# A two-block transformer kernel on one core: wider right sides for thin products, and an expert scatter in two passes, one block later

## What is computed

```python
for layer in range(DEPTH):
    mod = c @ w_ada[layer] + b_ada[layer]
    sh_a, sc_a, g_a, sh_f, sc_f, g_f = [m[:, None, :] for m in jnp.split(mod, 6, -1)]
    h = x * (1.0 + sc_a) + sh_a
    ...
    f = _swiglu(...) if layer % 2 == 0 else _moe(...)
    x = _layer_norm(DEEPNORM_ALPHA * x + (1.0 + g_f) * f, ln_g[layer, 1], ln_b[layer, 1])

def _moe(h, w_router, b_router, wg, wu, wd):     # top 2 of 8 experts, gates = their softmax
    ...
    for e in range(N_EXPERTS):
        out = out + gates[:, e:e + 1].astype(t.dtype) * _swiglu(t, wg[e], wu[e], wd[e])
```

## Time and profile before

| | |
|---|---|
| three runs | 2732.01, 2730.3, 2724.32 us; median 2730.3 |
| profiled execution | 2731.76 us; its span 2730.0 us |
| mean granted clock | 0.979 |
| PE, DVE, ACT busy | 97%, 80%, 56% |

### The profile page before, as it was taken

The page is one execution under the profiler, slowest core; times in us unless marked ns, Lnnn a source line. Parts: engine busy times, 40 slices in busy tenths (PEclk is TensorE's granted clock), DMA queues, the critical chain, the costliest instruction groups (busy, mean ns, idle before and its releaser), DMA issues.

```text
span 2730.0 us, 37737 instructions
## 1 busy us (share of the span) xinstructions
PE 2643.8 (97%) x15664; PEld 2346.4 (86%) x15664; DVE 2186.1 (80%) x2466; ACT 1519.5 (56%) x1567; POOL 50.8 (2%) x83
## 2 busy tenths in 40 slices
PE   6989999989999999999999999999999999999998
PEld 5879988878888888888888799998899999998898
DVE  6978767788888888888888889975487788954777
ACT  3533335557767777766777654544454554444554
POOL 2000000100000000000000000000000000000000
PEclk9989989989999999999999999999999998999999
DMA  8659954489999999999999953454555533444453
GB/s 315 228 203 328 359 203 162 120 311 369 356 342 360 347 356 353 359 348 353 350 356 350 330 178 109 146 173 142 174 193 189 172 115 132 155 154 169 156 186 116
DMA packets 376000, 669.85 MB, mean 245 GB/s; under 512 B 26761, under 2 KB 199439, under 8 KB 370959
## 3 DMA queue, kind: packets, MB, share of 16 engines
q1 hardware_dynamic: 358336, 662.55, 69.0%
q10 hardware_dynamic: 17487, 4.83, 0.7%
HBM read 663.13 MB, written 4.19 MB: 244 GB/s over the span
## 4 chain that ended last, share of the span: by engine, by line
PE 86%; DVE 8%; ACT 3%; issue 2%; DMA 1%; POOL 0%; ACTq 0%; DVEq 0%; POOLq 0%; SPq 0%
PE PS L444 24%; PE PS L446 24%; PE PS L445 24%; PE PS L544 2%; DVE LO L439 2%; DVE AR L721 2%; PE PS L2517 2%; PE PS L1674 2%; ACT HI L430 1%; DVE AR L2807 1%; PE PS L1911 1%; PE PS L1948 1%; PE PS L2403 1%; PE PS L2394 1%; PE PS L749 1%
## 5 line engine op out<-in xcount | busy, mean ns | idle before, releaser
L439 DVE TENSOR_TENSOR LO<-RAW,HI 128x2048 fp32r<-128x2048 f32 x410 | 930.6, 2274 | 221.2 <-ACT HI L430 220.8
L430 ACT ACTIVATE HI<-RAW 128x2048 fp32r<-128x2048 f32 x410 | 780.3, 1904 | 325.6 <-PE PS L446 287.2
L444 PE MATMUL PS<-X1H,HI 128*128 128x256 f32 (+1 forms) x2128 | 611.2, 287 | 7.2 <-DVE X1L L584 4.2
L445 PE MATMUL PS<-X1L,HI 128*128 128x256 f32 (+1 forms) x2128 | 605.2, 284 | 0.0
L446 PE MATMUL PS<-X1H,LO 128*128 128x256 f32 (+1 forms) x2128 | 604.8, 284 | 0.0
L444 PE MATMUL PS<-HI,X1H 128*128 128x512 f32 x1056 | 431.3, 408 | 0.9 <-DVE LO L439 0.4
L444 PEld LDWEIGHTS PS<-X1H,HI 128*128 128x128 f32 (+1 forms) x2128 | 409.4, 192 | 12.4 <-issue 9.8
L446 PE MATMUL PS<-HI,X1L 128*128 128x512 f32 x1056 | 413.8, 392 | 0.0
L445 PE MATMUL PS<-LO,X1H 128*128 128x512 f32 x1056 | 412.9, 391 | 0.0
L445 PEld LDWEIGHTS PS<-X1L,HI 128*128 128x128 f32 (+1 forms) x2128 | 409.4, 192 | 2.1
L446 PEld LDWEIGHTS PS<-X1H,LO 128*128 128x128 f32 (+1 forms) x2128 | 409.1, 192 | 0.8
(11 more groups left out here) (390 smaller groups left out, 2845.4 us busy)
## 6 DMA issues: line engine op xcount, KB each, us to landing
RAW<-in_w_in_dram SPq DMA_DIRECT2D x66, 1024.0 KB, 5.4
RAW<-in_expert_w_gate_dram SPq DMA_DIRECT2D x66, 1024.0 KB, 5.3
RAW<-in_expert_w_up_dram SPq DMA_DIRECT2D x64, 1024.0 KB, 5.3
RAW<-in_expert_w_down_dram SPq DMA_DIRECT2D x62, 1024.0 KB, 5.5
RAW<-in_ffn_w_up_dram SPq DMA_DIRECT2D x55, 1024.0 KB, 5.5
AR<-in_expert_w_down_dram SPq DMA_DIRECT2D x50, 1024.0 KB, 5.6
AR<-in_expert_w_up_dram SPq DMA_DIRECT2D x48, 1024.0 KB, 5.9
AR<-in_expert_w_gate_dram SPq DMA_DIRECT2D x46, 1024.0 KB, 5.5
```

Source lines behind the costliest of these rows:

```text
L430: a.activation(HI[:, n % NH, 0:size(i)], raw_at(i), ACT.Copy).then_inc(*hi.up(i))
L439: v.tensor_tensor(LO[:, m % NH, 0:n], raw_at(i), HI[:, m % NH, 0:n].bitcast(F32), ALU.subtract).then_inc(*lo.up(i))
L444: t.matmul(o, lh, rh, start=first, stop=False)
L445: t.matmul(o, lh, rl, start=False, stop=False)
```

## The change

`pe_ada_sum` takes all 128 columns of ones instead of one, and `gates` takes 128 columns of the tile `U` from where its 8 begin instead of those 8; the columns read are the first ones, as before. In the expert stage the gate values leave the one-hot matrix: only `PP` is built and turned (one buffer `PPT`, fp32r), the result `YE` (one buffer) is split into `YH` by ACT and `YL` by DVE, a quarter is two fp32r passes, and DVE multiplies with the gate value as it adds. The quarters move to blocks b = 2 to 5, the turn to the expert's own last block, and the hidden rows keep 2 slots instead of 3.

```diff
@@ pe_ada_sum
-            z = t.matmul(PS[:, bank, at + j:at + j + 1], SUMMED[n][:, 128 * j:128 * j + 128], ones[:, 0:1], start=True,
-                         stop=True)
+            z = t.matmul(PS[:, bank, at + j:at + j + 128], SUMMED[n][:, 128 * j:128 * j + 128], ones, start=True, stop=True)
@@ dve_select
-            v.tensor_scalar(PP[:, s_, k, :], iota, RP[:, k, x:x + 1], None, ALU.is_equal)
-            z = v.tensor_scalar(PG[:, s_, k, :], iota, RP[:, k, x:x + 1], GG[:, k, x:x + 1], ALU.is_equal, ALU.mult)
+            z = v.tensor_scalar(PP[:, s_, k, :], iota, RP[:, k, x:x + 1], None, ALU.is_equal)
@@ pe_turn, act_turn
+        t.wait_ge(*(dve_moe("gather", x + 1, 1) if x < 7 else dve_moe("scatter", 6, 3)))
+        turn(t, [(PS[:, 7, 128 * k:128 * k + 128], PP[:, x % 2, k, :]) for k in range(2)]).then_inc(*pe_moe.up("turn", x))
...
+        if x > 0:
+            a.wait_ge(*pe_moe("scatter", x - 1, 3))
+        a.activation(PPT[:, :], PS[:, 7, 0:256], ACT.Copy).then_inc(*act_moe.up("turn", x))
@@ pe_scatter
-        if q == 0:
-            t.wait_ge(*dve_moe("y", x))
-        if x < 7:
-            t.wait_ge(*(dve_moe("scatter", x, q - 1) if q else act_moe("turn", x + 1)))
-        t.matmul(PS[:, scatter_bank(x, q), :], PGT[:, x % 2, 128 * k:128 * k + 128], YE[:, x % 2, ns], start=True,
-                 stop=True).then_inc(*pe_moe.up("scatter", x, q))
+        if q == 0 or (x, q) == (7, 1):
+            t.wait_ge(*dve_moe("ylo", x, q if x == 7 else 1))
+            t.wait_ge(*act_moe("turn", x))
+        elif x < 7:
+            t.wait_ge(*dve_moe("scatter", x, q - 1))
+        places = PPT[:, 128 * k:128 * k + 128]
+        t.matmul(PS[:, scatter_bank(x, q), :], places, YH[:, ns], start=True, stop=False)
+        t.matmul(PS[:, scatter_bank(x, q), :], places, YL[:, ns], start=False, stop=True).then_inc(
+            *pe_moe.up("scatter", x, q))
@@ dve_scatter
-        v.tensor_tensor(X[:, k, ns], X[:, k, ns], PS[:, scatter_bank(x, q), :], ALU.add).then_inc(
-            *dve_moe.up("scatter", x, q))
+        v.scalar_tensor_tensor(X[:, k, ns], PS[:, scatter_bank(x, q), :], GG[:, k, x:x + 1], X[:, k, ns], ALU.mult,
+                               ALU.add).then_inc(*dve_moe.up("scatter", x, q))
@@ pe_between (dve_between the same)
-        if x > 0 and 1 <= b <= 4 and after == "g":
-            pe_scatter(t, x - 1, b - 1)
+        if x > 0 and 2 <= b <= 5 and after == "g":
+            pe_scatter(t, x - 1, b - 2)
...
-        if x < 7 and (b, after) == (6, "u"):
-            pe_turn(t, x + 1)
+        if (b, after) == (6, "u"):
+            pe_turn(t, x)
@@ act_hidden_moe (slots n % 3 become n % 2)
-        if n > 2:
-            a.wait_ge(*used(CH[f"moe{(n - 3) // 7}d"][2 * ((n - 3) % 7) + 1]))
+        if n > 1:
+            a.wait_ge(*used(CH[f"moe{(n - 2) // 7}d"][2 * ((n - 2) % 7) + 1]))
@@ act_moe_program
             if 0 < n < 56:
                 split_hi(a)
                 split_hi(a)
+                if b == 0:
+                    act_y(a, x - 1)
@@ dve_moe_program
             if x < NEXP:
                 split_lo(v)
+                if x > 0 and b == 1:
+                    dve_y_lo(v, x - 1)
@@ dve_y, act_y, dve_y_lo
-        if x > 1:
-            v.wait_ge(*pe_moe("scatter", x - 2, 3))
+        if x > 0:
+            v.wait_ge(*pe_moe("scatter", x - 1, 3))
...
+            v.tensor_tensor(YE[:, ns], PS[:, 5 + nb, :], GB2[:, ns], ALU.mult).then_inc(*dve_moe.up("y", x, nb))
+    def y_parts(x):
+        return ((0, slice(0, 512)), (1, slice(512, 1024))) if x == 7 else ((1, slice(0, 1024)),)
+    def act_y(a, x):
+        for nb, ns in y_parts(x):
+            a.wait_ge(*dve_moe("y", x, nb))
+            a.activation(YH[:, ns], YE[:, ns], ACT.Copy).then_inc(*act_moe.up("yhi", x, nb))
+    def dve_y_lo(v, x):
+        for nb, ns in y_parts(x):
+            v.wait_ge(*act_moe("yhi", x, nb))
+            v.tensor_tensor(YL[:, ns], YE[:, ns], YH[:, ns].bitcast(F32), ALU.subtract).then_inc(*dve_moe.up("ylo", x, nb))
@@ gates
-                    z = t.matmul(PS[:, 6 + k, 0:8], src[:, c % 4 if j == 2 else c, 128 * k:128 * k + 128],
-                                 WG[:, l, 8 * j + c, :], start=first and n == 0, stop=last and n == len(part) - 1)
+                    o = 192 * l + 8 * (8 * j + c)
+                    z = t.matmul(PS[:, 6 + k, 0:128], src[:, c % 4 if j == 2 else c, 128 * k:128 * k + 128],
+                                 U[:, o:o + 128], start=first and n == 0, stop=last and n == len(part) - 1)
```

More of the change, by code:

```diff
@@ L252, in emit_program @@
     WR = sb("WR", [128, 8, 8])
+    PPT = sb("PPT", [128, 256], F32R)
     PS = ctx.enter_context(nc.psum_tensor("PS", [128, 8, 512], F32))
@@ L1787, in emit_program @@
     m1, den2, CNT = ar(8272, 2), ar(8274, 2), ar(8280, 8)
-    PP, PG, PGT = ar(8448, 2, 2, 128), ar(8960, 2, 2, 128), ar(9472, 2, 256)
+    PP = ar(8448, 2, 2, 128)
     SGm, HFm = ar(9984, 2, 512), ar(11008, 2, 512)
-    YE = ar(12032, 2, 1024)
+    YE = ar(12032, 1024)
     GB2, LG2, LB2 = ar(14080, 1024), ar(15104, 1024), CST[:, C_DEC:C_DEC + 1024]
@@ L1795, in emit_program @@
     GL = X1L[:, :, :].rearrange("p a b -> p (a b)").rearrange("p (s c n) -> p s c n", s=2, c=8)
-    RHm = X2H[:, :, :].rearrange("p a b -> p (a b)").rearrange("p (s c n) -> p s c n", s=4, c=4)
-    RLm = X2L[:, :, :].rearrange("p a b -> p (a b)").rearrange("p (s c n) -> p s c n", s=4, c=4)
+    RHm = X2H[:, 0:4, :].rearrange("p a b -> p (a b)").rearrange("p (s c n) -> p s c n", s=2, c=4)
+    RLm = X2L[:, 0:4, :].rearrange("p a b -> p (a b)").rearrange("p (s c n) -> p s c n", s=2, c=4)
+    YH, YL = [t_[:, 4:8, :].rearrange("p a b -> p (a b)") for t_ in (X2H, X2L)]
     def pe_router(t):
@@ L1928, in pe_turn @@
     def pe_turn(t, x):
-        if x:
-            t.wait_ge(*dve_moe("gather", x, 1))
-        turn(t, [(PS[:, 7 if x else 6, 128 * k:128 * k + 128], PG[:, x % 2, k, :]) for k in range(2)]).then_inc(*pe_moe.up("turn", x))
+        t.wait_ge(*(dve_moe("gather", x + 1, 1) if x < 7 else dve_moe("scatter", 6, 3)))
+        turn(t, [(PS[:, 7, 128 * k:128 * k + 128], PP[:, x % 2, k, :]) for k in range(2)]).then_inc(*pe_moe.up("turn", x))
     def act_turn(a, x):
         a.wait_ge(*pe_moe("turn", x))
-        if x > 1:
-            a.wait_ge(*pe_moe("scatter", x - 2, 3))
-        a.activation(PGT[:, x % 2, :], PS[:, 7 if x else 6, 0:256], ACT.Copy).then_inc(*act_moe.up("turn", x))
+        if x > 0:
+            a.wait_ge(*pe_moe("scatter", x - 1, 3))
+        a.activation(PPT[:, :], PS[:, 7, 0:256], ACT.Copy).then_inc(*act_moe.up("turn", x))
     def scatter_bank(x, q):
@@ L1973, in act_between @@
             act_gather(a, x + 1, 1)
-        if x < 7 and (b, after) == (6, "u"):
-            act_turn(a, x + 1)
+        if (b, after) == (6, "u"):
+            act_turn(a, x)
     def dve_between(v, x, b, after):
-        if x > 0 and 1 <= b <= 4 and after == "g":
-            dve_scatter(v, x - 1, b - 1)
+        if x > 0 and 2 <= b <= 5 and after == "g":
+            dve_scatter(v, x - 1, b - 2)
         if x < 7 and (b, after) == (0, "g"):
@@ L1990, in pe_moe_program @@
         pe_gather(t, 0, 1)
-        pe_turn(t, 0)
         for n in range(7 * NEXP + 1):
@@ L2021, in pe_down @@
             if x > 0 and b == 0 and half == 0:
-                t.wait_ge(*dve_moe("y", x - 1))
+                t.wait_ge(*dve_moe("y", x - 1, 1))
             for nb, c in ((0, 0), (0, 1), (1, 0), (1, 1)):
                 ns, q = slice(512 * nb, 512 * nb + 512), 2 * half + c
-                z = mm3(t, PS[:, 5 + nb, :], RHm[:, n % 3, q, :], RLm[:, n % 3, q, :], hi_of(i)[:, c, ns],
+                z = mm3(t, PS[:, 5 + nb, :], RHm[:, n % 2, q, :], RLm[:, n % 2, q, :], hi_of(i)[:, c, ns],
                         lo_of(i)[:, c, ns], b == 0 and q == 0, b == 6 and q == 3)
@@ L2041, in act_hidden_moe @@
         a.wait_ge(*pe_moe("hid", n))
-        if n > 2:
-            a.wait_ge(*used(CH[f"moe{(n - 3) // 7}d"][2 * ((n - 3) % 7) + 1]))
-        a.activation(RHm[:, n % 3], PS[:, 4, :].rearrange("p (c n) -> p c n", c=4), ACT.Copy).then_inc(
+        if n > 1:
+            a.wait_ge(*used(CH[f"moe{(n - 2) // 7}d"][2 * ((n - 2) % 7) + 1]))
+        a.activation(RHm[:, n % 2], PS[:, 4, :].rearrange("p (c n) -> p c n", c=4), ACT.Copy).then_inc(
             *act_moe.up("hid", n))
@@ L2048, in dve_hidden_moe @@
         v.wait_ge(*act_moe("hid", n))
-        v.tensor_tensor(RLm[:, n % 3], PS[:, 4, :].rearrange("p (c n) -> p c n", c=4), RHm[:, n % 3].bitcast(F32),
+        v.tensor_tensor(RLm[:, n % 2], PS[:, 4, :].rearrange("p (c n) -> p c n", c=4), RHm[:, n % 2].bitcast(F32),
                         ALU.subtract).then_inc(*dve_moe.up("hidlo", n))
@@ L2058, in act_moe_program @@
         act_gather(a, 0, 1)
-        act_turn(a, 0)
         for n in range(7 * NEXP + 1):
@@ L2168, in emit_program @@
     WB2 = [ar(2048, 2048), ar(4096, 2048)]
-    P1, G1, GT1, Y1 = ar(8448, 2, 128), ar(8704, 2, 128), ar(8960, 256), ar(12032, 1024)
```

(16 more changed lines are left out.)

2 lines of the change are left out of this document (removed).

## The result

| | before | after |
|---|---|---|
| median time, 20 runs each | 2730.05 us | 2740.23 us |
| ratio, with its 95% interval | | 1.0034, 1.0026 to 1.0041 |
| span of the profiled execution | 2730.0 us | 2738.3 us |
| mean granted clock | 0.979 | 0.982 |
| PE busy | 2643.8 us | 2627.3 us |

What follows compares the result with a forecast made beforehand. PE was taken to bound the expert stage. Columns -9.7, new wait +14, clock with the stall +2 and last expert -0.5 gave +5.8 us on the profiled 2731.76; median forecast 2736 us, 8-in-10 range 2721 to 2748.

Steps and rivals of the forecast that it cites:

- The new wait: Expert boundaries: ACT's copy of the rows waits for DVE's product, PE idles before u1 and d0; +2.0 us each, +14.
- The clock with the stall: Expert boundaries: PE's clock may fall after the 2.4 us idle; 0.45 us at five of seven places, +2 us.
- The quarters: Expert stage: two fp32r passes replace each float32 quarter on PE; 1.65 us less per expert, 11.5 us less work.
- The last expert: End of expert stage: quarters wait for two short splits but are 1.6 us shorter; -0.5 us, bounds -1.6 and +1.5.
- The gate product: Gate product, twice: 128 columns keep PE's clock at 1.00; 2.7 us gained each, -5.4 us, bounds 2 and 10.
- The sums: Conditioning sums with 128 columns instead of one: wider passes cost nothing and can keep the clock up; -4.3 us together.
- sum 3: Third conditioning sum: PE's gain becomes a longer idle, after which the clock may fall; +1.4 us, bounds 0 and +1.7.
- sum 4: Fourth conditioning sum: PE would wait for DVE to read the sum, so only 0.6 us is gained; -0.6 us.
- sums 5 and 6: Fifth and sixth conditioning sums, 48 passes at 0.50: clock rises after the first 3.41 us; -5.1 us, bounds 0 and 5.1.
- The rival of the hidden wait: Expert boundaries: PE's u1 is not late, so the 11.5 and 9.7 us savings stand; 2709 us, chance 0.13.
- that of the columns which do nothing: Conditioning sums and gate product: 128 columns do not hold the clock, so they gain 0; 2746 us, chance 0.06.
- The rival of the clock: Seven expert boundaries: 0.50 follows each idle, the second idle absorbs nothing; 12 instead of 2 us, 2746 us, chance 0.16.

Runs made afterwards that it cites:

- the run with float32 quarters: Kernel before with only the four quarters moved one block later on PE and DVE, still float32: 2729.68 us, ratio 0.9999.
- the version with the latest copy: Changed kernel with ACT's copy of the expert's rows behind the splits after the SiLU, DVE's second part later too: 2712.08 us, ratio 0.9935.
- the run of the scatter alone: Changed kernel with conditioning sums and gate product set back to thin right sides, leaving only the expert-stage change: 2746.67 us, ratio 1.0067.

## Why the prediction was right, and where its sizes were off

The mechanism and the sign were right, and the sum was 3.5 us short of the 9.3 measured. By its steps:

- **The new wait** was forecast at +2.0 us an expert without the clock. Forecast was ACT held until 709.47; it was held until 708.33, and this trace enters the stage 1.1 us earlier, so the place is the same. Forecast were starts of u1 and d0 late by 2.4 and 1.2 us; the idle rows say 2.19 and 0.92. The forecast counts in the pace of starts; an idle row begins at the modelled end of the last pass, 0.16 us behind the place where the next start would fall, and the second start behind each idle comes after 0.34 us instead of 0.23 (713.57 to 713.91). In the pace that is 2.46 and 1.19 us, 3.65 in all, and less the 1.60 us of the quarters it is the 2.1 us by which an expert is longer at the four boundaries where the clock held. The copy of 1024 columns, taken as 1.03 us, took 1.06.
- **The clock with the stall** was +2, as 0.45 us at five boundaries. It fell at three, where the expert took 0.33 to 0.45 us more: +1.2. That the second idle absorbs most of the slow chunk is what both kinds of boundary show. The rival in which nothing is absorbed had 1.7 us at each and is out. Stage in all: 16.1 against 16.
- **The quarters** were forecast at 1.65 us less an expert; the version without any stall measured 1.60. Their place and the two slots for hidden rows cost nothing: the first by the run with float32 quarters, the second by the version with the latest copy, which has two slots. DVE's add with the gate values, priced as the plain add, takes 0.745 us instead of 0.681; DVE has the time.
- **The last expert** was -0.5, measured -1.1, inside its bounds.
- **The gate product** was -5.4. Alone on the chip it measured -6.2. The account of layer 0 was right up to the scan (3.0 forecast, 3.2 measured); the 0.3 us for the clock behind it was too little there, where a second slow stretch came, and -1.7 is left at copy 421. Layer 1 can't be told by itself: of the -4.9 in the ledger 3.1 to 4.8 also stand in traces with the thin product.
- **The sums** are the term that was mis-sized: -4.3 forecast, no gain measured (the run with sums alone, and thin against wide in the best version). At their place the steps were right: sum 3 (+1.4; measured +1.5, with an idle of 2.96 us behind it, near the 3.1 forecast, and 3.41 us at 0.50 behind that), sum 4 (-0.6; mostly -0.2 to -0.6), sums 5 and 6 (-5.1; measured -4.6 here, -4.9 in the run with sums alone). What the sum had no line for is what comes behind them: 2.7 us are given back by 521 us in both traces. I booked a gain of PE, in a stage where PE waits for DVE several times more, as if it ran through to the end. Waits of the changed kernel, 405 to 425 us:

```profile
PE PS L545 <- DVE X1L L603: 2.6, 1, 2.6
PE PS L545 <- DVE X L959: 2.4, 1, 2.4
```

The first of them was 2.3 us before, so 0.3 of the 2.7 us can be read there. Some 0.7 more is the place of the 6.8 us at 0.50 which both kernels have at 412 us: earlier by 1 us where the work is earlier by 3.3, it covers 5.98 us of PE's work instead of 4.55. And 1.6 are in the slow stretch shown at the end. Why the gain is given back in most traces and not in all stays open: part of it is where the stretches at 0.50 fall, which no run here controls.

Of the total's error of 3.5 us the sums make +4.3, the gate product and the last expert -1.4; the rest is within the interval of the ratio (7.1 to 11.2 us). That 5.8 came as near as it did owes something to these errors having opposite signs; the 16 us of the stage do not.

The rival of the hidden wait is out by the idle rows of PE above, that of the columns which do nothing by the run with the gate product alone. The rival of the clock had its condition wrong: an idle of 2.19 us was followed by 0.50 at three boundaries of seven, and the second idle took up most of the slow chunk. Two slips of the prediction change nothing: "every 128-column stretch at 1.00" overlooks eight passes of 128 columns from 415.96, inside the 6.8 us at 0.50, behind an idle; and its terms for slower add up to 0.44, not 0.42.

The Trainium skill's price of an isolated matmul by its columns (TensorE: Matmul & The Clock Gate, Back-to-back issue gap) doesn't describe these passes: 64 passes of 128 columns took 7.31 us, 0.114 each, where the page's 134 cycles against 60 would make the wide ones slower than the thin ones of 0.11.

## What to carry to other kernels

An instruction put into an engine's list is priced by what it waits for, not by how long it runs: the same 1.06 us copy made an expert 3.7 us longer in one place (127.22 us) than four chunks on (123.53), where it cost nothing that can be seen. Before such a wait goes into a list, look at where its releaser stands in the other list, and how much slack the work behind the wait has (here 1.6 us against 3.6). A gain of one engine counts in full only where that engine bounds what follows; where it waits for others again behind the gain, it may go there. And a step of 1 to 3 us read from one trace of each kernel is no effect yet: look whether a kernel without the edit has it too.

## What the runs showed that was not expected

The same idle is followed by a lower clock in one execution and not in another. At 512.65 us of before, PE has idled 1.14 us for DVE and goes on at 1.00; the changed kernel is 2.2 us earlier there, has the same passes and the same idle, and is at 0.50 from 510.76. The kernel with the quarters one block later runs the same program as before up to this place, and is at 0.50 from 514.06. Before, then after, then that kernel: timeline rows of PE and stretches of PE alone.

```profile
512.65 0.50 PE L444 MATMUL PS<-HI,X2H 128*128 128x512 f32 x1 [1.14 <-DVE AR L1521]
```
```profile
509.24:512.65 3.41, 2.27 (x21) 1.00 0.02 5
512.65:516.06 3.41, 3.41 (x15) 1.00 0.00 0
```
```profile
510.42 0.51 PE L445 MATMUL PS<-HI,X2H 128*128 128x512 f32 x1 [1.14 <-DVE AR L1521]
```
```profile
507.35:510.76 3.41, 2.27 (x20) 1.00 0.02 5
510.76:514.17 3.41, 3.41 (x10) 0.50 0.00 0
```
```profile
514.06 0.80 PE L444 MATMUL PS<-HI,X2H 128*128 128x512 f32 x1 [1.14 <-DVE AR L1521]
```
```profile
514.06:517.47 3.41, 3.41 (x8) 0.50 0.00 0
```

It costs 1.6 us (the step of the ledger there), and the run with the sums alone has it too, at 511.53. In all, five of the eight traces with wide sums have it and one of the five with thin ones. What decides isn't settled by these runs; they show that it is neither the length of the idle alone nor an edit further up, and five of eight against one of five is too little to say that wide sums make it likelier. In a sum of steps of 1 to 2 us such a stretch is as large as the steps. In the stage, an idle of 2.19 us was followed by 0.50 at three boundaries of seven, and at two of seven in the run of the scatter alone.
